# RWKV-7 scan of a hybrid diffusion step: the triangular inverse by fresh products, and products of one stationary joined to 128 columns

## The reference, cut to what matters

```python
def _rwkv_step(S, inp):
    r, w, kk, a, k, v = inp
    sk = jnp.einsum('bdhvk,bdhk->bdhv', S, kk)
    S = S * w[..., None, :] - sk[..., :, None] * (kk * a)[..., None, :] + v[..., :, None] * k[..., None, :]
    return S, jnp.einsum('bdhvk,bdhk->bdhv', S, r)
```

## Time and profile before

| | |
|---|---|
| time, median of 3 runs | 6053.59 us (6050.33 to 6060.71) |
| the profiled execution | 6041.68 us, span 6039.9 us |
| mean granted TensorE clock | 0.961 |
| TensorE busy | 5538.2 us, 92% |
| VectorE, ScalarE, POOL busy | 3316.2, 2205.1, 2219.7 us |
| the scans of the two layers | 292.87 and 294.68 us |

### The profile page before, as it was taken

How to read it: one execution, slowest core, us unless ns; L and a number is a source line. 1 busy time by engine, 2 the same in 40 slices (tenths; PEclk the granted TensorE clock), 3 DMA queues, 4 the chain that set the end, 5 groups by cost and what they waited for, 6 DMA issues and landing times. The chain is left out here.

```text
span 6039.9 us, 130192 instructions
## 1 busy us (share of the span) xinstructions
PE 5538.2 (92%) x53444; PEld 5352.4 (89%) x53444; DVE 3316.2 (55%) x6178; ACT 2205.1 (37%) x2717; POOL 2219.7 (37%) x1048
## 2 busy tenths in 40 slices
PE   5877897899999999999979688799999999999999
PEld 2757887899999999999968488699999999999999
DVE  4545547756565146566645465496555541656655
ACT  4433222355555622222224332224555564222221
POOL 0002222365566543343300032225556564334332
PEclk8988998999999999999989799899999999999999
DMA  5200012245555565445411000224555556554553
GB/s 200 81 34 13 5 59 84 96 164 177 175 176 182 165 220 174 163 165 175 142 71 51 19 7 17 84 69 135 177 174 180 176 168 226 167 170 163 170 167 111
DMA packets 304063, 778.41 MB, mean 129 GB/s; under 512 B 23724, under 2 KB 109228, under 8 KB 299496
## 3 DMA queue, kind: packets, MB, share of 16 engines
q1 hardware_dynamic: 303592, 771.81, 37.9%
HBM read 586.38 MB, written 185.34 MB: 128 GB/s over the span
## 5 line engine op out<-in xcount | busy, mean ns | idle before, releaser
L2135 POOL TENSOR_TENSOR ex_v_lo<-ex_v_raw,ex_v_hi 128x1024 fp32r<-128x1024 f32 x256 | 692.1, 2724 | 1071.4 <-ACT ex_v_hi L2041 1071.4
L335 PE MATMUL ex_ps<-tk_h_hi,tk_u_hi 128*128 128x320 f32 x4096 | 966.4, 317 | 44.0 <-POOL tk_u_lo L2123 34.8
L2123 POOL TENSOR_TENSOR tk_u_lo<-tk_u_raw,tk_u_hi 128x1024 fp32r<-128x1024 f32 x256 | 655.5, 2561 | 883.2 <-ACT tk_u_hi L2011 870.5
L335 PE MATMUL ex_ps<-ex_wa_hi,ex_v_hi 128*128 128x320 f32 x4096 | 935.1, 310 | 18.8 <-issue 18.8
L335 PE MATMUL ex_ps<-tk_h_hi,tk_u_lo 128*128 128x320 f32 x4096 | 938.3, 310 | 3.8 <-issue 3.8
L335 PE MATMUL ex_ps<-tk_h_lo,tk_u_hi 128*128 128x320 f32 x4096 | 937.0, 310 | 0.0
L335 PE MATMUL ex_ps<-ex_wa_hi,ex_v_lo 128*128 128x320 f32 x4096 | 934.8, 309 | 0.0
L335 PE MATMUL ex_ps<-ex_wa_lo,ex_v_hi 128*128 128x320 f32 x4096 | 934.7, 309 | 0.0
L2295 DVE TENSOR_TENSOR ex_y<-ex_y,ex_ps 128x640 f32<-128x640 f32 x496 | 405.9, 818 | 671.4 <-PE ex_ps L335 666.7
L335 PEld LDWEIGHTS ex_ps<-tk_h_hi,tk_u_hi 128*128 128x128 f32 x4096 | 680.0, 190 | 46.1 <-POOL tk_u_lo L2123 35.7
L335 PEld LDWEIGHTS ex_ps<-ex_wa_hi,ex_v_hi 128*128 128x128 f32 x4096 | 686.5, 188 | 19.3 <-issue 19.3
(11 more groups left out here) (341 smaller groups left out, 8333.9 us busy)
## 6 DMA issues: line engine op xcount, KB each, us to landing
tk_u_raw<-in_expert_u SPq DMA_DIRECT2D x256, 512.0 KB, 4.2
ex_v_raw<-in_expert_v SPq DMA_DIRECT2D x256, 512.0 KB, 3.6
act_spill<-tk_act_e SPq DMA_DIRECT2D x256, 320.0 KB, 2.3
grid_scratch<-tk_grid SPq DMA_DIRECT2D x160, 512.0 KB, 5.4
ex_g<-grid_scratch SPq DMA_DIRECT2D x64, 1280.0 KB, 11.0
x<-in_w_mod_rows SPq DMA_DIRECT2D x192, 256.0 KB, 4.6
ex_a<-act_spill SPq DMA_DIRECT2D x32, 1280.0 KB, 7.8
x<-act_spill SPq DMA_DIRECT2D x32, 1280.0 KB, 8.0
```

Of the source, the lines that this page charges most:

```text
L335: ins = nc.tensor.matmul(out[:, q, 0:HALF], a, b[:, q * HALF:(q + 1) * HALF], start=(first and n == 0), stop=(last and n == 2))
L2123: nc.gpsimd.tensor_tensor(u_lo[:, at % 2], u_raw[:, at % 3], u_hi[:, at % 2].bitcast(F32), ALU.subtract).then_inc(e["u_split"], 1)
L2135: nc.gpsimd.tensor_tensor(v_lo[h][:, k], v_raw[:, k], v_hi[h][:, k].bitcast(F32), ALU.subtract).then_inc(e["v_split"], 1)
```

## The change

The inverse is built in another way. X starts as I plus the signed part that joins pairs of tokens, and UT as the transpose of I minus L (POOL adds the I). A level is two fresh products, Q = UT'X and its transpose form X'UT; VectorE cuts Q with a mask that keeps the joining corners and the diagonal and writes the new X (`corner`, double-buffered in X0 and X1), ScalarE copies the other one back to UT (`turned`). There are 6 levels with the first, the last without the transpose; a last mask gives M. Then M is applied from the left to the pair (b, F) instead of to a and q1: `wf` holds both results side by side, so all products that follow with one stationary operand are joined to 128 columns: the pair products a.(b, k) and b.(a, r), M.(nb, F), a_tok'.wf (A and r in one), PT'.wf (subtracted from kT and GT together, `kg`). B and Y0 become one product each, and the state's product s accumulates on B and ys on Y0 in PSUM. The transposes move from the front into levels 0 to 2. POOL's five level masks go; it keeps one addition of I and `rk`. ScalarE's `decays` now stand after `turned` of levels 4 and 5, VectorE's `ab` after `corner` of levels 3 and 4. The masks are 11 instead of 10 of 64 x 64 a direction.

The diff, cut (the setup of tiles, the masks' values and unchanged waits are left out):

```diff
-N_MASKS = 3 + LEVELS
+N_MASKS = 5 + LEVELS
...
+            def turned(st, i, lv):
+                act.wait_ge(st.e["qt_done"], (LEVELS - 1) * i + lv)
+                nc.scalar.activation(st.UT, st.ps[:, 1, :].rearrange("p (j t) -> p j t", t=CHUNK),
+                                     ACT.Copy).then_inc(st.e["ut_ready"], 1)
...
             for i in range(TILES):
                 for lv in range(1, LEVELS):
                     for st in streams:
-                        take_x(st, i, lv)
-                    if lv in (2, 3) and i + 1 < TILES:
-                        decays(streams[lv - 2], i + 1)
+                        turned(st, i, lv)
+                    if lv <= 3:
+                        for st in streams:
+                            tokens(st, i, lv, (st.a_tok, st.nf[:, :, 0, :], st.kg[:, :, 0, :])[lv - 1], (1.0, -1.0, 1.0)[lv - 1])
+                    elif i + 1 < TILES:
+                        decays(streams[lv - 4], i + 1)
                 for st in streams:
+                    act.wait_ge(st.e["wf_done"], i + 1)
+                    nc.scalar.activation(st.wf[:, 0:RB].rearrange("p b n t -> p (b n t)"), st.ps[:, 0, :],
+                                         ACT.Copy).then_inc(st.e["w_low"], 1)
...
-                for lv in range(1, LEVELS):
-                    for st in streams:
-                        level_mask(st, i, lv)
+                    pool.wait_ge(st.e["ut_cut"], i + 1)
+                    nc.gpsimd.tensor_tensor(st.UT, st.UT, st.ident, ALU.add).then_inc(st.e["ut_ready"], 1)
...
+            def corner(st, i, lv):
+                dve.wait_ge(st.e["q_done"], LEVELS * i + lv)
+                cut(st.X[lv % 2], one_bank(st, 0), st.mask4(5 + lv), st.e["x_ready"])
...
                 for st in streams:
+                    e = st.e
+                    dve.wait_ge(e["ap_done"], i + 1)
+                    cut(st.X0, by_head(st, 0, 0), st.mask4(5), e["x_cut"])
+                    dve.wait_ge(e["lf_done"], i + 1)
+                    cut(st.UT, by_head(st, 2, 0), st.mask4(0), e["ut_cut"])
+                    dve.wait_ge(e["x_cut"], i + 1)
+                    v.tensor_tensor(st.X0, st.X0, st.ident, ALU.add).then_inc(e["x_ready"], 1)
                 for st in streams:
+                    cut(st.PT, by_head(st, 0, 1), st.mask4(3), st.e["p_taken"])
+                    cut(st.nf[:, :, 1, :], by_head(st, 2, 1), st.mask4(1), st.e["f_taken"])
                 for st in streams:
+                    dve.wait_ge(st.e["kr_done"], i + 1)
+                    cut(st.kg[:, :, 1, :], by_head(st, 2, 0), st.mask4(2), st.e["kr_taken"])
                 for lv in range(1, LEVELS):
                     for st in streams:
+                        corner(st, i, lv)
+                    if lv in (3, 4) and i + 1 < TILES:
+                        ab(streams[lv - 3], i + 1)
                 for st in streams:
+                    dve.wait_ge(st.e["q_done"], LEVELS * i + LEVELS)
+                    cut(st.M, one_bank(st, 0), st.mask4(4), st.e["m_ready"])
                 for st in streams:
+                    dve.wait_ge(st.e["wf_done"], i + 1)
+                    v.tensor_copy(st.wf[:, RB:HEADS].rearrange("p b n t -> p (b n t)"), st.ps[:, 1, :]).then_inc(st.e["w_high"], 1)
+                for st in streams:
+                    dve.wait_ge(st.e["pw_done"], i + 1)
+                    dve.wait_ge(st.e["kr_taken"], i + 1)
+                    v.tensor_tensor(twin_pairs(st.kg), twin_pairs(st.kg), whole(st), ALU.subtract).then_inc(st.e["kg_ready"], 1)
+                for st in streams:
+                    dve.wait_ge(st.e["a_taken"], i + 1)
                     v.tensor_tensor(st.rr.rearrange("p b (c t) -> p c b t", c=2),
+                                    st.ps[:, 2:4, :].rearrange("p c (b n t) -> p c b n t", n=2, t=CHUNK)[:, :, :, 1, :],
                                     st.rT.rearrange("p b (c t) -> p c b t", c=2), ALU.add).then_inc(st.e["r_taken"], 1)
+
...
+                    advance(st, 0)
+                for st in streams:
+                    decay(st, 0)
+                for st in streams:
+                    advance(st, 1)
                 for st in streams:
                     dve.wait_ge(st.e["ys_done"], 2 * i + 2)
+                    if st.d:
+                        dve.wait_ge(streams[0].e["ys_taken"], i + 1)
+                    elif i:
+                        dve.wait_ge(streams[1].e["ys_taken"], i)
+                    y = s.x[:, 4:8, token(st, i)].rearrange("p b (c t) -> p c b t", c=2)
+                    v.tensor_tensor(y, by_head(st, 2, 0), y, ALU.add).then_inc(st.e["ys_taken"], 1)
+                for st in streams:
+                    decay(st, 1)
...
+            def pair_products(st, bank, left, right):
+
+                for b in range(RB):
+                    for h, c in quads:
+                        last = mm(st.ps[rows(c), bank + h, :].rearrange("p (n b t) -> p n b t", n=2, b=RB)[:, :, b, :],
+                                  left[rows(h), b, rows(c)], right[rows(h), :, b, rows(c)], start=(b == 0),
+                                  stop=(b == RB - 1))
+                return last
...
+            def twin_product(st, left, right):
+
+                for j, c in chunks():
+                    last = mm(st.ps[rows(c), j // RB, P * (j % RB):P * (j % RB) + P], left[rows(c), j, :],
+                              right[rows(c), j].rearrange("p n t -> p (n t)"), start=True, stop=True)
+                return last
...
+                    pair_products(st, 0, st.aT, st.bk).then_inc(e["ap_done"], 1)
...
+                    pair_products(st, 2, st.bT, st.ar).then_inc(e["lf_done"], 1)
...
+                    pe.wait_ge(st.e["f_taken"], i + 1)
+                    pe.wait_ge(st.e["ut_cut"], i + 1)
+                    pair_product(st, 2, st.kT, st.rT).then_inc(st.e["kr_done"], 1)
+                for lv in range(LEVELS):
                     for st in streams:
                         e = st.e
+                        pe.wait_ge(e["x_ready"], LEVELS * i + lv + 1)
+                        pe.wait_ge(e["ut_ready"], LEVELS * i + lv + 1)
+                        if lv == 0:
+                            pe.wait_ge(e["p_taken"], i + 1)
+                        chunk_product(st, 0, st.UT, st.X[lv % 2]).then_inc(e["q_done"], 1)
+                        if lv < LEVELS - 1:
+                            chunk_product(st, 1, st.X[lv % 2], st.UT).then_inc(e["qt_done"], 1)
                     for st in streams:
+                        if lv == 0:
+                            pe.wait_ge(st.e["kr_taken"], i + 1)
+                        if 1 <= lv <= 2:
+                            pe.wait_ge(st.e["tr_taken"], 3 * i + lv)
+                        if lv <= 2:
+                            to_tokens(st, (st.aT, st.bT, st.kT)[lv])
                 for st in streams:
+                    pe.wait_ge(st.e["m_ready"], i + 1)
+                    pe.wait_ge(st.e["f_taken"], i + 1)
+                    pe.wait_ge(st.e["tr_taken"], 3 * i + 3)
+                    twin_product(st, st.M, st.nf).then_inc(st.e["wf_done"], 1)
                 for st in streams:
+                    pe.wait_ge(st.e["w_low"], i + 1)
+                    pe.wait_ge(st.e["w_high"], i + 1)
+                    for b in range(RB):
+                        for h, c in quads:
+                            j = h * RB + b
+                            last = mm(st.ps[rows(h), 2 + c, P * b:P * b + P], st.a_tok[rows(c), j, :],
+                                      st.wf[rows(c), j].rearrange("p n t -> p (n t)"), start=True, stop=True)
+                    last.then_inc(st.e["ar_done"], 1)
+                    twin_product(st, st.PT, st.wf).then_inc(st.e["pw_done"], 1)
                 for st in streams:
+                    pe.wait_ge(st.e["kg_ready"], i + 1)
+                    for b in range(RB):
+                        for h, c in quads:
+                            j = h * RB + b
+                            last = mm(st.ps[rows(h), c, rows(b)], st.kg[rows(c), j, 0, :], value(st, i, c, j),
+                                      start=(b == 0), stop=False)
+                    last.then_inc(st.e["b_done"], 1)
                 for st in streams:
                     pe.wait_ge(st.e["r_taken"], i + 1)
+                    for b in range(RB):
+                        for h, c in quads:
+                            j = h * RB + b
+                            last = mm(st.ps[rows(h), 2 + c, rows(b)], value(st, i, c, j), st.kg[rows(c), j, 1, :],
+                                      start=(b == 0), stop=False)
+                    last.then_inc(st.e["y0_done"], 1)
...
```

More of the change, by code:

```diff
@@ L1076, in ab, with cut, one_bank, whole @@
                 v.tensor_tensor(st.bT, st.W_inv, st.kka[:, :, token(st, i)], ALU.mult).then_inc(e["ab_ready"], 1)
[L1078 to L1099, removed]
-            links[0].n += 1
+            def cut(dst, src, mask, done):
+                v.tensor_tensor(pairs(dst), src, mask, ALU.mult).then_inc(done, 1)
```

(43 more changed lines are left out.)

257 lines of the change are left out of this document (58 added, 199 removed).

## The result

The changed kernel takes 6089.86 us, the median of four runs (6084.29 to 6096.29), beside 6052.61 for the kernel before on the same chip: a ratio of 1.0059, with a 95% interval of 1.0042 to 1.0077. It is slower, by some 37 us. The forecast was 6082, in a range of 6035 to 6108. Of all executions behind this text one was slow, a run of experiment 3 with 8154.19 us at a mean granted clock of 0.64, and the ratios leave it out.

The account below looks back on a forecast made before the run. TensorE's work plus issue gaps bounded the scan. Tiles summed to 286.2 us a layer, with 20.4 of clock drops 615.0 for two against 587.6; with masks 28 us slower, so 6082 us, range 6035 to 6108.

Parts of the forecast that it names:

- The stalls: Levels: TensorE waits 4.5 us twice a tile, in four tiles, for VectorE's corner held behind ab and late decays.
- The collision of the copy with POOL: Inside each stall: VectorE's 8-column copy takes 0.81 us beside POOL's kT; without it the stall would be 3.9 us.
- Rival 2: Levels: the stalls don't come; 72 us faster, 5982 us; chance 0.14.
- The clock: Scan: TensorE's idle gaps in fronts and levels bring half clock, 1.7 us each, 12 a layer, 20.4 us.
- Rival 1: Scan: the stalls come but the clock holds; 13 us faster, 6041 us; chance 0.20.
- rival 3: Scan: the clock stays low twice as long, 12 x 3.4 us a layer; 68 us slower, 6122 us; chance 0.13.
- Front and tail: Ends of an ordinary tile: front 9.0 us against 13.0, bound by VectorE; tail 16.4 us against 18.3.
- The joined products: Scan: joining cuts TensorE instructions from 1944 to 1368 a tile but saves no streaming; a joined product counts as two halves.
- the issue gaps: Fast four-quadrant stretches: TensorE's unexplained idle gaps, 5.9 us a tile, should go with wider instructions.
- Rival 4: Scan: joined products are split again or issue gaps stay at 6 us a tile; 60 us over the forecast; chance 0.05.
- eight transposes: Levels: three pairs of transposes moved from the front add 3 x 0.87 us a tile.
- the first tile: Start of the scan: 7.7 us longer than an ordinary tile, kept unchanged from before, its slow clock start included.

Follow-up runs that it names:

- experiment 3: Changed kernel with four spare products that nobody reads run by TensorE in each stall: 6055.2 us, ratio 1.0005 to the kernel before.
- Experiment 1: Changed kernel with ScalarE's decays for the next tile back after its copies of levels 2 and 3: 5987.42 us, ratio 0.9896 to the kernel before.
- experiment 2: Kernel before the change with ScalarE's decays moved from levels 2 and 3 to 4 and 5: 6080.45 us, ratio 1.0046.
- experiment 5: Changed kernel with POOL's kT and rT of the next tile held until VectorE's ab is ready: 6071.93 us, ratio 1.0029 to the kernel before.
- experiment 4: Changed kernel with each product of 128 moving columns split into two of 64: 6132.82 us, ratio 1.0133 to the kernel before.

## Why the prediction was right

**The stalls** were the step that decided, and they came as worked out: 4.5 us forecast, 4.47 measured from 684.06 to 688.53, in front of the products behind the corners of levels 4 and 5, in the four tiles with a next one and not in the last. The last tile's addition to y comes 50.6 us after the one before it, with 48.5 plus one drop of 1.7 forecast; the ordinary ones take 62.2, 64.1 and 62.2, with 57.5 plus 5.1 forecast. Experiment 1 shows the order of the decays as the cause, experiment 2 that it acts on the old algebra too. The collision of the copy with POOL, 0.64 us each by experiment 5, was inside the term, as the prediction had it. Rival 2, no stalls at all, was priced at 5982 us; experiment 1, which takes them away, has 5987.

**The clock.** Forecast: twelve drops a scan beside the slow start, 1.7 us each. The clock records have these twelve in each scan, eight at the stalls and four at the fronts, and a thirteenth in the first front. The price was low: 1.9 to 2.2 us for a stall's (experiments 1 and 3). Rival 1, a clock that holds, is out; rival 3, a price of 3.4 us, is out too, though ten of the 26 drops do last 6.8 us. The third tile has two of these at its stalls, and is 1.9 us longer for it than its neighbours; its levels take 38.1 us, where the sum had 32.1 and two drops of 1.7. The granted clock came out lower than the 0.92 forecast, at 0.89 and 0.88. The Trainium skill, TensorE: Matmul & The Clock Gate, section "HAM oscillation — how this bites in real kernels", says that a wait in every turn of a loop can bring the half clock back in every turn; the drop at each of the sixteen stalls agrees.

**Front and tail.** 9.0 forecast, 9.3 measured; 16.4 forecast, 16.6 measured. VectorE is the front's bound, as its row says: 8.49 of 9.33 us busy. The wait there is for the last f cuts, as forecast:

```profile
662.56 0.69 PE L1169 MATMUL rw_ps<-rw_ar,rw_bk 64*64 64x64 f32 x32 [3.54 <-DVE rk L1063]
...
663.75 1.13 PE L1169 MATMUL rw_ps<-rw_ar,rw_bk 64*64 64x64 f32 x32 [0.50 <-DVE rk L1063]
```

The last k by r product takes 0.91 us, from 663.75 to the first product of level 0 at 664.66, where 0.47 was forecast: the clock records have a drop from 663.4 on. That is the 0.3 us.

**The joined products.** That the issue gaps go was right (25.7 us in the first scan to none), and experiment 4 brings 14.2 of them back by splitting. Rival 4 put this at 6 us a tile, from the third tile alone; the mean over the scan before was 5.1, and undoing the joining cost 43 us in all, not 60. That "joining saves instructions but no streaming" was nearly right: a wide product of a stream takes 1.74 us, from 643.82, where I counted 1.87; with four of them a tile the streaming gain is 0.5 us a tile. By luck it was given back in one place that I had priced too low, from the front: eight transposes take 1.03 us inside the levels (669.45 to 670.48), not 0.87, three times a tile, 0.5 us a tile again.

**What was off.** The profiled execution took 6084.3 us, the sum said 6070. Of the 14 us, 11.2 are in the scans and 3 outside (4 less the 0.8 forecast for the masks), which is within the spread of the runs. In the first scan the miss is 5.2 us, and 4.1 of it lie in the first tile, whose start I had taken over unchanged (7.7 us above an ordinary tile): from the first decay to the end of its y are 72.7 us, where the sum had 68.6. The clock records show a drop of 3.4 us at 537.1, in that first front, beside the slow start; I had counted the first front as free. The first tile's two stalls have drops of 6.8 us like the third tile's, which cost that one 1.9 us. The rest is the price of a drop. So the mechanisms held, and the mis-sized terms are the drop (1.7, measured about 2) and the first tile.

The forecast's sign hung on the clock, and that was its weak side: with it at 1.7 us a gap the scans were 27 us longer, without it 13 us shorter. The rows of before had one gap with a drop and one without, so that the price was above 0.5 us was a choice, and in that part the sign was luck. The runs put the balance so: the new algebra with its joined products gains 61.5 us in the scans (experiment 1 against the kernel before, 526.1 against 587.6), the stalls take 68.8 back, and the clock behind them 31.

## What to carry to other kernels

When a change moves a producer's step behind another one (here ScalarE's exponentials behind two copies), walk the queue of its consumer: what stands behind the consumer in the same queue is late as well, and here it was the operation that the bottleneck engine waits for. A stall of 4.5 us in front of TensorE cost some 6.5 here, since half clock came with it; repeated 16 times that was more than a good change of algebra had gained, and moving one condition gave it back. And look in stretches of very short instructions (14.6 ns here) for gaps that no wait in the program explains: fewer and wider instructions removed them.

## What the runs showed of the hardware

- Each of the sixteen waits of 4.3 us in front of TensorE had a drop to half clock, of 3.4 or 6.8 us, that began between 1.9 us before the wait's end and 0.2 us behind it. In experiment 2 six of eight waits of 2.4 us had one of 3.4 us, and none of eight waits of 0.7 us.
- Useless products in a stall saved time: experiment 3 issues 2048 more instructions (16 x 128), is 35 us faster, and has 5 drops a scan instead of 13.
- Stretches of 64-column products on four quadrants, 14.6 ns an instruction, had issue gaps (25.7 us a scan before, 14.2 in experiment 4); with 128-column ones between them there were at most 0.9 us of them a scan. Why the supply fails there stays open: the profile names only "issue", and no run here took the gaps apart.
- Beside a POOL operation of 128x512, VectorE's copy of 8 columns took 0.81 us instead of 0.17. It ended with POOL's operation: at 687.28, where that ended at 687.25, so the copy seems to wait for it. VectorE's cut of 128x512 at 659.42, with POOL's addition of I beside it (658.99 to 660.64), stayed at 0.68. POOL's addition of I took 1.65 us beside VectorE's work in the front, against 1.27 for its `kT` in the stall; whether VectorE is the cause was not tried.
